# Two-block network on one core: norm sums and inverses in PSUM banks, another order in the first attention and in the second front

## The reference

```python
def rmsnorm(x, g):
    y = xf * lax.rsqrt(jnp.mean(xf * xf, axis=-1, keepdims=True) + EPS)
...
h = modulate(rmsnorm(x, norm1_g), shift, scale)      # norm (layer, 1)
p = h @ w_in                                          # GLU, q, k, v and gate columns
y_conv = conv_branch(p_glu, ...)                      # GLU, depthwise conv with 31 taps, layernorm, silu, w_o
y_attn = neighbourhood_attention(q, k, v, k_ctx, v_ctx, rpb)   # 8 heads; context_attention in layer 0
x = x + gate * gated_merge(p_gate, y_conv, y_attn, w_o)
h = modulate(rmsnorm(x, norm2_g), shift2, scale2)     # norm (layer, 2)
x = x + gate2 * conv_ffn(h, w_up, dw, dw_b, w_down)
```

## Time and profile before

| | us |
|---|---|
| median of three runs | 1931.9 (1930.01 to 1933.9) |
| the profiled execution | 1932.97 |
| its span in the trace | 1931.0 |
| TensorE busy in it | 1887.8 (98%) |
| VectorE, ScalarE, GpSimd busy | 996.8, 893.6, 1164.6 |

### The profile page before, as it was taken

One profiled execution on the slowest core, in us unless ns is written; L12 is line 12 of the kernel. 1 busy time (PEld: TensorE's weight loads), 2 busy tenths in 40 slices (PEclk: granted clock), 3 DMA queues, 4 the chain that ended last, 5 costly groups with the idle time before them and its releaser, 6 DMA issues.

```text
span 1931.0 us, 33248 instructions
## 1 busy us (share of the span) xinstructions
PE 1887.8 (98%) x12120; PEld 1611.5 (83%) x12120; DVE 996.8 (52%) x1974; ACT 893.6 (46%) x1520; POOL 1164.6 (60%) x904
## 2 busy tenths in 40 slices
PE   7999999999999999999999999999999999999998
PEld 4677777888888887877889999887999998779987
DVE  4879746353443324888645534776442038655400
ACT  4223444243433323525546645546554355555533
POOL 2444232533544554735469988673788876649986
PEclk9999999999999999999999999999999999999999
DMA  9942233728433343426465575432455564326553
GB/s 387 365 126 87 59 97 109 243 81 180 137 109 107 113 150 130 141 87 205 161 217 177 184 239 179 165 117 82 145 183 181 179 205 136 110 72 212 197 174 131
DMA packets 121541, 306.98 MB, mean 159 GB/s; under 512 B 29640, under 2 KB 51528, under 8 KB 121044
## 3 DMA queue, kind: packets, MB, share of 16 engines
q1 hardware_dynamic: 118808, 300.98, 46.9%
q10 hardware_dynamic: 2620, 4.44, 1.5%
HBM read 300.65 MB, written 8.06 MB: 160 GB/s over the span
## 4 chain that ended last, share of the span: by engine, by line
issue 38%; POOL 32%; PE 27%; DVE 1%; ACT 1%; DMA 0%; POOLq 0%; ACTq 0%; DVEq 0%
POOL w_lo L810 32%; PE bank L1385 6%; PE bank L1390 6%; PE bank L1386 6%; PE bank L2145 2%; PE bank L2144 2%; PE bank L2146 2%; PE bank L2013 1%; PE bank L2015 1%; PE bank L2014 1%; DMA tab<-in_tables 0%; PE bank L2257 0%; DVE v_lo L2330 0%; PE bank L2044 0%; ACT w_hi L853 0%
## 5 line engine op out<-in xcount | busy, mean ns | idle before, releaser
L810 POOL TENSOR_TENSOR w_lo<-raw,w_hi 128x512 fp32r<-128x512 f32 x884 | 1146.6, 1326 | 752.9 <-ACT w_hi L853 752.5
L853 ACT ACTIVATE w_hi<-raw 128x1024 fp32r<-128x1024 f32 x442 | 466.2, 1057 | 286.9 <-PE bank L1390 160.2
L1385 PE MATMUL bank<-h_hi,w_hi 128*128 128x256 f32 (+1 forms) x1248 | 404.1, 340 | 1.8 <-DVE h_lo L2330 1.1
L1386 PE MATMUL bank<-h_lo,w_hi 128*128 128x256 f32 (+1 forms) x1248 | 396.1, 334 | 0.0
L1385 PEld LDWEIGHTS bank<-h_hi,w_hi 128*128 128x128 f32 x1248 | 235.0, 188 | 42.9 <-issue 13.2
L1390 PE MATMUL bank<-h_hi,w_lo 128*128 128x256 f32 (+1 forms) x1248 | 261.3, 333 | 0.0
L1386 PEld LDWEIGHTS bank<-h_lo,w_hi 128*128 128x128 f32 x1248 | 235.3, 189 | 23.6 <-issue 0.2
L1390 PEld LDWEIGHTS bank<-h_hi,w_lo 128*128 128x128 f32 x1248 | 203.0, 189 | 24.1
L1385 PE MATMUL bank<-u_hi,w_hi 128*128 128x272 f32 (+1 forms) x736 | 211.2, 287 | 0.6 <-POOL w_lo L810 0.6
L1390 PE MATMUL bank<-u_hi,w_lo 128*128 128x272 f32 (+1 forms) x736 | 208.7, 284 | 0.0
L1386 PE MATMUL bank<-u_lo,w_hi 128*128 128x272 f32 (+1 forms) x736 | 207.2, 281 | 0.0
(11 more groups left out here) (401 smaller groups left out, 3587.6 us busy)
## 6 DMA issues: line engine op xcount, KB each, us to landing
raw<-in_wstream SPq DMA_DIRECT2D x442, 512.0 KB, 3.5
ada_raw<-in_wada SPq DMA_DIRECT2D x48, 512.0 KB, 12.9
late_a<-in_wada SPq DMA_DIRECT2D x16, 512.0 KB, 4.7
late_b<-in_wada SPq DMA_DIRECT2D x16, 512.0 KB, 4.5
biash<-rpb_by_offset SPq DMA_DIRECT2D x64, 64.0 KB, 2.4
gates<-in_wada SPq DMA_DIRECT2D x8, 512.0 KB, 4.8
rpb_by_offset<-in_rpb SPq DMA_DIRECT2D x16, 224.0 KB
bias_by_distance<-vec ACTq DMA_DIRECT2D x1, 3264.0 KB
```

What stands on the lines that cost most here:

```text
L810: i = pool.tensor_tensor(lo[:, part, s, :], whole[:, part, :], hi[:, part, s, :].bitcast(F32), ALU.subtract)
L853: act.activation(w_hi[q >= first["l2", 0]][:, :, s, :], raw[:, s, :].rearrange("p (g c) -> p g c", c=PAIR), ACT.Copy)\
L1385: pe.matmul(o, tile(w_hi, i, k), a_hi, start=start, stop=False)
L1386: pe.matmul(o, tile(w_hi, i, k), a_lo, start=False, stop=False)
```

## The change

Six edits. (1) Three norms, (1, 1), (0, 2) and (1, 2), add their squares up in a PSUM bank instead of `rinv`, the last addition goes to `rinv`, and their reciprocal lies in bank 4, from where the multiplies read it. (2) Gate tile 0 of the attention has bank 7 instead of bank 0. (3) In the first pair of heads VectorE does head 0's probabilities ahead of head 1's maxima, and the two taps between them join the five behind. (4) In layer 1 the tap groups of two and three have one tap more. (5) The layernorm behind the convolution has its reciprocal in bank 5 and its tanh in banks 6 and 7. (6) In the second front the first `u` comes behind index heads 2 and 3 and each later `u` one step later, on VectorE and ScalarE.

```diff
+sq_total = {(1, 1): bank[0], (0, 2): aux[2], (1, 2): aux[2]}
...
     L1_PLAN += [("mean", 0)] * last + [("gate", 4 * p + 3), ("Tc", o)]
-    VECTOR1_PLAN += [("Sx", e, o), ("Sc", e)] if p else [("Sx", o)]
-    VECTOR1_PLAN += [("tap", 2), ("Tx", e), ("Tc", e)] + V_
+    if p:
+        VECTOR1_PLAN += [("Sx", e, o), ("Sc", e), ("tap", 2), ("Tx", e), ("Tc", e)] + V_
+    else:
+        VECTOR1_PLAN += [("Tx", e), ("Sx", o), ("Tc", e), ("tap", 2)]
...
 TAPS_BANK = 2
+
+def gate_bank(n):
+
+    return n % 2 if n else 7
...
-U_BEHIND = [("slab", KCR), ("index", 3), ("index", 5), ("index", 7)]
+U_BEHIND = [("index", 3), ("index", 5), ("index", 7), ("vals", 1, 2)]
...
 SCALAR_PLAN.append(("lam", 0))
-VECTOR_PLAN = [("rho", 0), ("stream", 0), ("wi", 0), ("index", 0), ("index", 1), ("tabs", 0), ("u", 0)]
-VECTOR_PLAN += [("index", 2), ("index", 3), ("u", 1), ("rope", QCR), ("index", 4), ("index", 5), ("u", 2)]
-VECTOR_PLAN += [("rope", QCR + 1), ("index", 6), ("index", 7), ("u", 3), ("rope", KCR), ("rope", KCR + 1), ("lam", 0)]
+VECTOR_PLAN = [("rho", 0), ("stream", 0), ("wi", 0), ("index", 0), ("index", 1), ("tabs", 0), ("index", 2), ("index", 3)]
+VECTOR_PLAN += [("u", 0), ("rope", QCR), ("index", 4), ("index", 5), ("u", 1), ("rope", QCR + 1), ("index", 6), ("index", 7)]
+VECTOR_PLAN += [("u", 2), ("rope", KCR), ("rope", KCR + 1), ("u", 3), ("lam", 0)]
...
                 act.wait_ge(*after("norm_summed" if summed else "norm_added", (tag, c - 2)))
-            dst = rinv[:, 0:T] if not summed and c == 0 else sq[:, c % 2, 0:T]
+            dst = sq_total.get(tag, rinv)[:, 0:T] if not summed and c == 0 else sq[:, c % 2, 0:T]
...
                 act.wait_ge(*after("chunk", (layer, "gate", n)))
-                act.activation(gates[:, n, 0:T], lin[n % 2][:, 0:T], ACT.Tanh, scale=0.5)\
+                act.activation(gates[:, n, 0:T], bank[gate_bank(n)][:, 0:T], ACT.Tanh, scale=0.5)\
...
                 act.wait_ge(*after("conv_affine", (layer, c)))
-                act.activation(sq[:, c % 2, 0:T], nb[:, c, 0:T], ACT.Tanh).then_inc(*done("conv_tanh", (layer, c)))
+                if 2 <= c:
+                    act.wait_ge(*after("conv_silu", (layer, c - 2)))
+                act.activation(aux[2 + c % 2][:, 0:T], nb[:, c, 0:T], ACT.Tanh).then_inc(*done("conv_tanh", (layer, c)))
...
             norm_sum((layer, 1), T_BOTH, False, late="between")
+            readers[4] = ("normed", ((1, 1), DC - 1, 1))
...
             if kind == "gate":
-                chunk(s + n, n % 2, T, h_hi, h_lo, (layer, "gate", n), ("gate_out", (layer, n)))
+                chunk(s + n, gate_bank(n), T, h_hi, h_lo, (layer, "gate", n), ("gate_out", (layer, n)))
...
                         .then_inc(*done("ln_var", (layer, c)))
-                readers[5] = ("ln_root", layer)
+                readers[5] = ("conv_scaled", (layer, CONV_C - 1))
...
         norm_sum((layer, 2), T, False, late=("mixed", "mixed1")[layer], behind=(0, 4)[layer])
+        readers[4] = ("normed", ((layer, 2), DC - 1, parts(layer)[-1][0]))
...
             readers[m] = ("down_out", (layer, m))
+        if layer == 0:
+            readers[0] = ("norm_added", ((1, 1), DC - 1))
...
                 dve.wait_ge(*after("norm_root", tag))
-                dve.reciprocal(rinv[:, cols], rinv[:, cols]).then_inc(*done("norm_rinv", (tag, st)))
+                dve.reciprocal(inverse_[:, cols], rinv[:, cols]).then_inc(*done("norm_rinv", (tag, st)))
...
             dve.wait_ge(*after("scale1_ready", (layer, 1)))
-            norm((layer, 1), X, T_BOTH, h_hi, h_lo, scale(a1), shift(0), parts(0)[0:1])
+            norm((layer, 1), X, T_BOTH, h_hi, h_lo, scale(a1), shift(0), parts(0)[0:1], inverse_=aux[0])
...
             if layer:
-                norm((layer, 1), X, T_BOTH, h_hi, h_lo, scale(a1), shift(0), parts(0)[1:2], True, (2 * c, 2 * c + 1))
+                norm((layer, 1), X, T_BOTH, h_hi, h_lo, scale(a1), shift(0), parts(0)[1:2], True, (2 * c, 2 * c + 1), aux[0])
...
             elif kind == "tap":
-                tap(h if h else len(taps))
+                tap(h + (layer if h < 5 else 0) if h else len(taps))
...
-        inverse(rinv[:, 0:T], "ln_root", "ln_rstd", layer)
+        dve.wait_ge(*after("ln_root", layer))
+        dve.reciprocal(aux[1][:, 0:T], rinv[:, 0:T]).then_inc(*done("ln_rstd", layer))
+        dve.wait_ge(*after("ln_rstd", layer))
...
                 v = nb[:, c, 0:T]
-                stt(v, cv[:, c, 0:T], par(layer, "lng", c), rinv[:, 0:T], ALU.mult, ALU.mult)\
+                stt(v, cv[:, c, 0:T], par(layer, "lng", c), aux[1][:, 0:T], ALU.mult, ALU.mult)\
...
                 dve.wait_ge(*after("conv_tanh", (layer, c - 1)))
-                stt(v, sq[:, (c - 1) % 2, 0:T], 1.0, v, ALU.add, ALU.mult).then_inc(*done("conv_silu", (layer, c - 1)))
+                stt(v, aux[2 + (c - 1) % 2][:, 0:T], 1.0, v, ALU.add, ALU.mult).then_inc(*done("conv_silu", (layer, c - 1)))
...
             if m >= 2:
-                norm_add((layer, 2), m - 1, T)
+                norm_add((layer, 2), m - 1, T, aux[2])
...
                     .then_inc(*done("scale2_ready", 1))
-        norm_add((layer, 2), DC - 1, T)
+        norm_add((layer, 2), DC - 1, T, aux[2], rinv)
...
             dve.wait_ge(*after("scale2_ready", 1))
-        norm((layer, 2), X, T, h_hi, h_lo, scale(a2), shift(3 * DC), parts(layer))
+        norm((layer, 2), X, T, h_hi, h_lo, scale(a2), shift(3 * DC), parts(layer), inverse_=aux[0])
...
             if m >= 2 and not eager:
-                norm_add(tag, m - 1, T_BOTH)
+                norm_add(tag, m - 1, T_BOTH, bank[0])
...
             eager_lo(0, DC - 1)
-        for m in range(1 if eager else DC - 1, DC):
-            norm_add(tag, m, T_BOTH)
+        if eager:
+            for m in range(1, DC):
+                norm_add(tag, m, T_BOTH)
+        else:
+            norm_add(tag, DC - 1, T_BOTH, bank[0], rinv)
```

## The result

The changed kernel took 1935.22 us (median of 20 runs, 1931.46 to 1937.92) against 1931.63 for the kernel before, timed beside it (20 runs, 1927.39 to 1938.56). The ratio is 1.0021, with a 95% interval of 1.0014 to 1.0029: 3.6 us slower by the medians, 4.1 by the ratio. I had forecast 1929.6 within 1925.0 to 1933.0.

A forecast was written before the change was run, and what follows sets the result against it. TensorE bounds the kernel, busy 1887.8 us of 1931.0, leaving 43 us idle. The terms 1.8 + 1.2 + 1.1 - 0.2 - 1.6 give 2.3 us gained, from the median of 1931.9 to 1929.6, range 1925.0 to 1933.0.

The forecast's parts named there:

- Norm sums and inverse: Layer 1's two norms: operands in PSUM shorten VectorE's work and TensorE's stalls near 808 and 1000; gains 1.8 and 1.2.
- Second front: Near 1231: relu of index heads 2 and 3 no longer behind a rounding, so TensorE's wait for `score` goes; gain 1.1.
- Layer 0, first pair: Seven taps in one run on VectorE meet GpSimd more, three or four of them slow; loss 1.6 us.
- the second rival: TensorE idles some 3 us in layer 0, bringing a low-clock stretch costing 1.7; gain 0.6, 1931.3 us; 15 in 100.
- Layer 1, first pair: With gate tile 0: TensorE reaches head 1's transposes earlier, then waits for `sq`; nothing, bounds -0.5 and +0.5.
- Layer 1, taps: One tap more per group: loss 1.0 in pairs 1 and 2, gain 0.8 in the last pair; loss 0.2.
- Gate tile and convolution norm: Gate tile 0 no longer waits for `v_out`; the convolution norm's multiplies run uncontested by GpSimd; both nothing.
- The fourth rival: Layer 0: four taps each wait for a whole GpSimd subtraction; loss 5.1 against gains of 3.9, 1933.1 us; 8 in 100.
- The third: Norm stalls of 1.80 and 1.84 go, but another releaser stands right behind; 1931.9 or 1933.5 us; 10 in 100.

The follow-up runs named there:

- only_multiply_l0: The kernel before with the first pair's new VectorE order (head 0's probabilities ahead of head 1's maxima) in layer 0 alone; ratio 1.0020 to the kernel before.
- undo_multiply: The changed kernel with the first pair's old VectorE order put back in both layers, all else kept; ratio 0.9990 to the kernel before.
- only_norms: The kernel before with the three norms' sums and inverses in PSUM banks alone; ratio 0.9986 to the kernel before.
- taps_first: The kernel before with one tap more in the first group of layer 1's first pair alone; ratio 1.0001 to the kernel before.

## Why the prediction was wrong

- **Norm sums and inverse (gains of 1.8 and 1.2).** Right, and the size fits: 2.7 us alone (1.0 to 4.4), both stalls gone, the root behind its table load.
- **Second front (1.1).** The wait went as forecast; the time is under what the runs can tell.
- **Layer 0, first pair (loss 1.6).** The step that failed. The work and the contention were right: the run of taps took 9.24 us with four slow taps, and the second half of the transposes came 1.6 later than before, 1.9 less the 0.3 by which the execution was ahead. What failed is the end of it: the term stopped at the arrival of `sq`. The wait in front of it had become one of 3.88 us, and the clock was low for 6.8 to 10 us behind it, which the term put at nothing. That more than doubles the loss: only_multiply_l0 costs 3.9 us (1.9 to 5.8). I had this as the second rival, at 15 in 100, and set against it that the clock had not fallen after 1.35 us of waiting. But that wait is gone in the new order and a longer one stands elsewhere; the row did not speak of it. It was also one execution: behind the same wait the clock fell in undo_multiply's. The Trainium skill ("TensorE: Matmul & The Clock Gate", section "HAM oscillation — how this bites in real kernels") tells of waits that drop the clock again and again. The trace agrees, with 0.50 behind 3.88 us. The prediction called the rival likely by that section and still left its cost out of the sum. I also priced it at one stretch, 1.7, where two to three came.
- **Layer 1, first pair ("nothing").** The waits add up to about the same, as I said, but not their lengths: one of 1.21 and short ones became one of 2.62, with the clock low behind it, which cost 1.4 in that execution (+1.7 to +3.1 in the table). I moved idle time about as if it had no price by length.
- **Layer 1, taps (loss 0.2).** The rows moved as forecast (0.2 lost in the trace). The time says 3 alone and 4.8 taken out of the changed kernel; the cause is open, and with it a large part of the distance between forecast and time.
- **Gate tile and convolution norm (nothing).** Not contradicted one by one; together they may gain.
- **The fourth rival** (the taps block fully) did not come: 9.24 us is below its 11.3. The third did not either.

## What to carry to other kernels

Idle time on TensorE is not additive: before an order is changed, add up how long the waits are where they end up, and price a gathered one with a stretch at the low clock behind it. Here 3.9 us brought it in four executions of four, waits under 2 us in four of fifteen; one execution in which the clock stayed up behind a wait says little. Look in each run at the mean granted clock beside the time. An operand moved from SBUF to PSUM pays where GpSimd works beside it and a stall ends on the instruction, and both can be read before.

## What the runs showed of the hardware

The same matmuls run at two speeds in whole stretches at the full clock. In layer 1's FFN the changed kernel's execution and that of only_norms have (stretches, first of each):

```profile
1034.00:1058.00 24.00, 24.00 (x206) 24.00 (x205) 13.34 (x30) 15.93 (x27) 21.77 (x19) 1.00 0.59 194
```

```profile
1030.00:1054.00 24.00, 24.00 (x214) 24.00 (x213) 13.74 (x31) 15.65 (x26) 22.89 (x19) 1.00 0.61 198
```

That is 206 against 214 matmuls in 24 us, with TensorE busy throughout; over the stretch of some 115 us it is 4.0 us. The kernel before has the slow speed there in its profiled execution. Of the 17 executions with the same TensorE instructions 6 have the fast one, 4.0 us ahead from 1012 to 1128, and none lies between. The stretches from 1130 to 1190 and behind 1756 also show two speeds, 2.0 to 2.5 us apart. What picks the speed was not tried. It is as large as most effects here, and may be one reason why runs of one kernel lie up to 15 us apart (taps_first, 1928.64 to 1943.32).
